# HGRN2 layer of a RetNet/S5/HGRN2 hybrid: the final output projection is woven into the last HGRN steps, and the decode heads into the second half's strips

## The reference, cut to what matters

```python
z = h @ w_in                                   # 1024 -> 4 * 1024: q, f_raw, i, g
q = silu(q)
f_gate = lower_bound + (1 - lower_bound) * sigmoid(f_raw)
log_f, k = log(f_gate), 1 - f_gate
o, s_new = hgrn2_chunkwise(q, log_f, k, i, s_hg)   # per head: s = diag(decay) s + k^T i, o = q s
o = head_rms_norm(o, norm_w) * silu(g)
x = x + o @ w_out                              # w_out1, 1024 x 1024
y = rms_norm(x, final_norm_w)
```

## Time and profile before

| | us |
|---|---|
| runs (3), median | 3449.12 |
| runs, lowest to highest | 3437.54 to 3450.01 |
| the profiled execution, its own time | 3435.53 |
| its span in the trace | 3433.7 |
| PE busy | 3118.8 (91%) |
| DVE, ACT, POOL busy | 1441.1, 1060.1, 1021.2 |

### The profile page before, as it was taken

One profiled execution on the slowest core, in us unless ns is written; L12 is line 12 of the kernel. 1 busy time (PEld: TensorE's weight loads), 2 busy tenths in 40 slices (PEclk: granted clock), 3 DMA queues, 4 the chain that ended last, 5 costly groups with the idle time before them and its releaser, 6 DMA issues. The chain is left out here.

```text
span 3433.7 us, 46623 instructions
## 1 busy us (share of the span) xinstructions
PE 3118.8 (91%) x16972; PEld 2750.7 (80%) x16972; DVE 1441.1 (42%) x2894; ACT 1060.1 (31%) x1761; POOL 1021.2 (30%) x641
## 2 busy tenths in 40 slices
PE   6999899899999688597899969999989999967799
PEld 6999899688888575497788849999978888866587
DVE  7998344214410596533300022133444444455522
ACT  4111122312211241433200020034545454588221
POOL 2232222122223472111222202344434444433021
PEclk9999999899999898799899979999989999967899
DMA  5444655455532563443422222333333333332342
GB/s 133 98 130 138 184 165 159 104 131 169 169 114 86 209 208 112 166 123 119 158 93 95 86 94 76 99 124 111 111 109 116 113 115 99 95 132 67 141 160 99
DMA packets 376296, 429.97 MB, mean 125 GB/s; under 512 B 49600, under 2 KB 318400, under 8 KB 366960
## 3 DMA queue, kind: packets, MB, share of 16 engines
q1 hardware_dynamic: 258960, 347.81, 32.4%
q10 hardware_dynamic: 117216, 80.53, 7.5%
HBM read 281.07 MB, written 151.39 MB: 126 GB/s over the span
## 5 line engine op out<-in xcount | busy, mean ns | idle before, releaser
L1114 PE MATMUL p_psum<-p_h_hi,p_w_hi 128*128 128x344 f32 (+1 forms) x1600 | 568.3, 355 | 0.0
L1114 PE MATMUL p_psum<-p_h_hi,p_w_lo 128*128 128x344 f32 (+1 forms) x1600 | 562.0, 351 | 0.0
L1114 PE MATMUL p_psum<-p_h_lo,p_w_hi 128*128 128x344 f32 (+1 forms) x1600 | 560.9, 351 | 0.0
L2328 PE MATMUL p_psum<-p_h_hi,p_w_hi 128*128 128x344 f32 (+1 forms) x1280 | 461.9, 361 | 0.0
L2328 PE MATMUL p_psum<-p_h_lo,p_w_hi 128*128 128x344 f32 (+1 forms) x1280 | 455.5, 356 | 0.0
L2328 PE MATMUL p_psum<-p_h_hi,p_w_lo 128*128 128x344 f32 (+1 forms) x1280 | 455.2, 356 | 0.0
L698 POOL CAST p_w_hi<-p_w_raw 128x1024 fp32r<-128x1024 f32 x80 | 88.9, 1112 | 821.0 <-PE p_psum L1114 685.4
L1114 PEld LDWEIGHTS p_psum<-p_h_hi,p_w_hi 128*128 128x128 f32 x1600 | 302.8, 189 | 36.7 <-issue 9.5
L1114 PEld LDWEIGHTS p_psum<-p_h_hi,p_w_lo 128*128 128x128 f32 x1600 | 302.8, 189 | 29.1
L1114 PEld LDWEIGHTS p_psum<-p_h_lo,p_w_hi 128*128 128x128 f32 x1600 | 302.8, 189 | 28.5
L2137 DVE COPY p_out<-p_psum 128x344 f32<-128x344 f32 (+1 forms) x160 | 93.4, 584 | 481.8 <-PE p_psum L2328 481.7
(11 more groups left out here) (321 smaller groups left out, 5605.7 us busy)
## 6 DMA issues: line engine op xcount, KB each, us to landing
p_w_raw<-in_w_in SPq DMA_DIRECT2D x144, 512.0 KB, 4.5
z<-p_out ACTq DMA_DIRECT2D x64, 512.0 KB, 3.5
z<-p_out SPq DMA_DIRECT2D x64, 512.0 KB, 3.2
p_raw<-z SPq DMA_DIRECT2D x32, 1024.0 KB, 5.4
rt_raw<-z SPq DMA_DIRECT2D x16, 1536.0 KB, 6.9
c_m_raw<-m SPq DMA_DIRECT2D x16, 1024.0 KB, 6.8
u_s<-p_out SPq DMA_DIRECT2D x128, 73.0 KB, 3.1
p_shared<-u_s SPq DMA_DIRECT2D x32, 292.0 KB, 5.1
```

The lines of the kernel that those rows point to most:

```text
L1114: ins = pe.matmul(bank, wv[par][:, k, :], h[:, k, c0:c0 + n], start=(k == 0 and j == 0), stop=(k == KD - 1 and j == 2))
L2328: ins = pe.matmul(bank, wv[par][:, k, :], h[:, k, c0:c0 + n], start=(k == 0 and j == 0), stop=(k == KD - 1 and j == 2))
```

## The change

The two last stages become one function; `combine` is no longer called for the second layer.

- The strips of the second half use PSUM banks 0 and 1 only, and a block waits for the eviction of the same block of the strip just before it. Banks 2 and 3 are free for the decode heads.
- The 8 decode heads move into the iterations 10 to 20, one new head in each, its parts spread over three iterations. Their states go through four buffers (the token buffers `xt` and `xn`, which the second half's prelude has left) instead of eight. DVE gets one head's work per iteration, PE its 2 transposes, 8 products into states and 8 out of them. SP loads and stores a state per iteration; before, ACT's queue stored them.
- At iteration 23 (`LAST_STRIP`) `w_out1` is loaded and split into the memory of the split tokens (`h_hi`, `h_lo`), through four row buffers: POOL makes the high parts, DVE the low parts. POOL also splits the first two input tiles.
- From iteration 25 (`OUT`) each iteration computes one tile of the output projection, `out_part(c, 0)` where strip `slot(k, 0)` was and `out_part(c, 1)` where `slot(k, 1)` was. So 9 tiles share iterations 25 to 33 with the HGRN steps and 8 follow in iterations 34 to 41. DVE's `add_out` comes after `norm_o`, ACT's `square_out` after `square_o`, DVE's `norm_out` at the end of the iteration; POOL's `split_mixed` does both parts of the input; SP loads tile c+2 and stores the result.
- `log_f` has one buffer instead of two.

```diff
+        s_state = [v[:].rearrange("p (n c) -> p n c", c=P) for v in (xt[0], xt[1], xn[0], xn[1])]
+        k_own = wrow[0:NS].rearrange("p (n c) -> p n c", c=P)
...
+        wo_hi, wo_lo = h_hi[:, :, 0:D], h_lo[:, :, 0:D]
+        wo_raw = [v[:, 0:D] for v in (out_buf[0], out_buf[1], xn[0][:], xn[1][:])]
+        m_raw, m_hi, m_lo = w_raw, w_hi, w_lo
+        xi, xo, sq = xt, xn, [o[:, 0:D] for o in out_buf]
...
+        OWN, OWN_END, OUT = 10, 20, 25
+        N_OUT = NT + 1
...
+            def load_weights(r):
+                if r >= 4:
+                    sp.wait_ge(wo_lo_done, r - 3)
+                sp.dma_start(wo_raw[r % 4], a["w_out1"][r * P:(r + 1) * P, :]).then_inc(wo_ld[r % 4], 16)
+            def load_mixed(c):
+                tile, n = out_no(c)
+                if c >= 2:
+                    sp.wait_ge(m_lo_done, c - 1)
+                if c < NT:
+                    for u in range(2):
+                        at = tile // NTH * (2 * NTH) + u * NTH + tile % NTH
+                        sp.wait_ge(mix_st[at % 2], 16 * (at // 2 + 1))
+                sp.dma_start(m_raw[c % 2][:, :, 0:n], mix["z"][tile, :, :, :] if n == P else mix["zs"])\
+                    .then_inc(m_ld[c % 2], 16)
+                if c >= 2:
+                    sp.wait_ge(sum_done, c - 1)
+                sp.dma_start(xi[c % 2][0:n, :], x_in["x"][tile, :, :] if n == P else x_in["s"]).then_inc(xi_ld[c % 2], 16)
+            def store_out(c):
+                tile, n = out_no(c)
+                sp.wait_ge(y_done, c + 1)
+                sp.dma_start(x_out["x"][tile, :, :] if n == P else x_out["s"], xo[c % 2][0:n, :]).then_inc(y_st[c % 2], 16)
...
+                    if k == LAST_STRIP and e == 0:
+                        sp.wait_ge(blk_done, blocks_to(N_STRIPS))
+                        for e4 in range(4):
+                            sp.wait_ge(s_st[e4], 32)
                         for par in range(2):
                             sp.wait_ge(stored[par], store_count(N_STRIPS + par))
-                        for h in range(HH):
...
+                        sp.wait_ge(w_lo_done, N_STRIPS)
+                        for r in range(4):
+                            load_weights(r)
+                        for c in range(2):
+                            load_mixed(c)
+                        for r in range(4, KD):
+                            load_weights(r)
+                    if e == 1 and out_tile(k) is not None and out_tile(k) + 2 < N_OUT:
+                        if out_tile(k) + 2 == NT:
+                            sp.wait_ge(d_stored, 16)
+                        load_mixed(out_tile(k) + 2)
+                    if e == 0 and out_tile(k - 1) is not None:
+                        store_out(out_tile(k - 1))
...
+                if k == LAST_STRIP:
+                    pool.wait_ge(blk_done, blocks_to(N_STRIPS))
+                    for r in range(KD):
+                        pool.wait_ge(wo_ld[r % 4], 16 * (r // 4 + 1))
+                        pool.tensor_copy(wo_hi[:, r, :], wo_raw[r % 4]).then_inc(wo_hi_done, 1)
+                        if r < 2:
+                            split_mixed(r)
+                elif out_tile(k) is not None and out_tile(k) + 2 < N_OUT:
+                    split_mixed(out_tile(k) + 2)
...
+            def square_out(c):
+                par, n = c % 2, out_no(c)[1]
+                act.wait_ge(sum_done, c + 1)
+                if c == 0:
+                    act.wait_ge(wo_lo_done, KD)
+                act.activation(sq[par][0:n, :], xo[par][0:n, :], ACT.Square, scale=D ** -0.5,
+                               accum_out=stat[par][0:n, 0:1]).then_inc(ysq_done, 1)
+                act.wait_ge(ysq_done, c + 1)
+                act.activation(stat[par][0:n, 1:2], stat[par][0:n, 0:1], ACT.Sqrt, bias=eps[0:n, :]).then_inc(yrms_done, 1)
...
+            for k in range(OUT + N_OUT + 1):
                 if k == BEFORE_B:
                     prelude(1)
                 if 0 <= k - 1 < N_HG:
                     values(k - 1)
-                if k >= 2:
...
+                if 0 <= k - 2 < N_HG:
                     square_o(k - 2)
+                if out_tile(k - 1) is not None:
+                    square_out(k - 1 - OUT)
                 if k < N_HG:
                     exps(k)
                 if 0 <= k - 1 < N_HG:
                     turned_keys(k - 1)
                 if k + 1 < N_HG:
-                    log_gates(k + 1)
...
+                    log_gates(k + 1, k == OWN - 2)
...
-                    dve.tensor_copy(out_buf[par][:, c0:c0 + n], ps[:, b if hf == 0 else 2 * par + b, 0:n])\
+                    dve.tensor_copy(out_buf[par][:, c0:c0 + n], ps[:, b, 0:n])\
...
+            def own_keys(h):
+                dve.wait_ge(own_mm, h + 1)
+                if h:
+                    dve.wait_ge(kv_mm, 2 * h)
+                dve.tensor_copy(i_own[:], ps_own[0:NS, 0, :])
+                dve.tensor_tensor(k_own, bcast(ps_own[0:NS, 1, :], 1, NS), bcast(ident[0:NS, 0:NS], 2, P), ALU.mult)\
+                    .then_inc(own_done, 1)
+                s = s_state[h % 4]
+                dve.wait_ge(s_ld[h % 4], 16 * (h // 4 + 1))
+                dve.tensor_tensor(s, s, bcast(own_f[:, h // H4, h % H4, :], 2, P), ALU.mult).then_inc(dec_done, 1)
+            def add_own(h, c):
+                s = s_state[h % 4][:, 4 * c:4 * c + 4, :]
+                dve.wait_ge(dec_done, h + 1)
+                dve.wait_ge(kv_mm, 2 * h + c + 1)
+                dve.tensor_tensor(s, s, ps_kv, ALU.add).then_inc(kv_done, 1)
...
+            for k in range(OUT + N_OUT + 1):
                 if k == BEFORE_B:
                     prelude(1)
-                if k >= 2:
+                if 0 <= k - 2 < N_HG:
                     take_state(k - 2)
                 if k < N_HG:
                     relative(k)
-                if k >= 2:
+                if 0 <= k - 2 < N_HG:
                     norm_o(k - 2)
+                if own_head(k - 1) is not None:
+                    add_own(k - 1 - OWN, 0)
...
+                if out_tile(k - 1) is not None:
+                    add_out(k - 1 - OUT)
                 evict(slot(k, 0), (0, 1, 2))
                 if 0 <= k - 1 < N_HG:
                     mask_scores(k - 1)
-                if k >= 2:
+                if 0 <= k - 2 < N_HG:
                     mix_o(k - 2)
                 if k < N_HG:
                     queries(k)
...
+                if own_head(k - 1) is not None:
+                    add_own(k - 1 - OWN, 1)
+                if own_head(k) is not None:
+                    own_keys(k - OWN)
...
                 evict(slot(k, 1), (0, 1))
                 if k + 1 < N_HG:
                     sum_logs(k + 1)
                 evict(slot(k, 1), (2,))
-
...
+                if k == LAST_STRIP:
+                    for r in range(KD):
+                        dve.wait_ge(wo_hi_done, r + 1)
+                        dve.tensor_tensor(wo_lo[:, r, :], wo_raw[r % 4], wo_hi[:, r, :].bitcast(F32), ALU.subtract)\
+                            .then_inc(wo_lo_done, 1)
+                if out_tile(k - 1) is not None:
+                    norm_out(k - 1 - OUT)
...
-                    if hf == 0:
-                        before = blocks_to(g - 1) + b + 1 if g else 0
-                    else:
-                        before = blocks_to(g - 2) + b + 1 if s >= 2 else blocks_to(N_P1)
+                    before = blocks_to(g - 1) + b + 1 if g else 0
                     if before:
                         pe.wait_ge(ev_done, before)
-                    bank = ps[:, b if hf == 0 else 2 * par + b, 0:n]
+                    bank = ps[:, b, 0:n]
...
+            def out_part(c, half):
+                par, n = c % 2, out_no(c)[1]
+                if half == 0:
+                    pe.wait_ge(wo_lo_done, KD)
+                    pe.wait_ge(m_lo_done, c + 1)
+                    if c == 0:
+                        pe.wait_ge(ev_done, blocks_to(N_STRIPS))
+                    if c == 1:
+                        pe.wait_ge(dmix_done, 1)
+                    if c >= 2:
+                        pe.wait_ge(sum_done, c - 1)
+                for k in range(KD):
+                    for j, (m, w) in enumerate(((m_hi, wo_hi), (m_hi, wo_lo), (m_lo, wo_hi))):
+                        ins = pe.matmul(ps[0:n, 2 * par + half, :], m[par][:, k, 0:n],
+                                        w[:, k, half * BLK:(half + 1) * BLK],
+                                        start=(k == 0 and j == 0), stop=(k == KD - 1 and j == 2))
+                if half:
+                    ins.then_inc(mm_done, 1)
...
+            for k in range(OUT + N_OUT):
                 if k == BEFORE_B:
                     prelude(1)
                 strip(slot(k, 0))
+                if out_tile(k) is not None:
+                    out_part(k - OUT, 0)
                 if 0 <= k - 1 < N_HG:
                     turn_k(k - 1)
                     scores(k - 1)
-                if k >= 2:
+                if 0 <= k - 2 < N_HG:
```

(13 more changed lines are left out.)

349 lines of the change are left out of this document (195 added, 154 removed).

## The result

The kernel after takes **3384.17 us** (median of 4 runs, 3382.68 to 3388.75). The kernel before, timed beside it on the same chip, takes 3443.33 (3437.01 to 3450.01). The ratio is 0.983 (95% interval 0.9803 to 0.9857). The forecast was 3384, in 3354 to 3418. The profiled executions tell less of a gain than the medians: their spans are 3386.9 and 3433.7 us, 46.8 apart against 59 between the medians. The executions of the kernel before come near 3434 or near 3447 us (10 and 14 of the 24 that were timed beside the first experiments), the profiled one is of the first kind, and the traces put the difference into one stretch, the decode heads' products behind the last step.

A forecast was written before the change was run, and what follows sets the result against it. PE was taken to bound iterations with strips, ACT those without, and PE the last stage. Saving 99.7 less 34 for heads gave about 65: 3370.5 us profiled, plus 13.6 to the median, 3384; range 3354 to 3418.

The forecast's parts named there:

- From iteration 23 to the end: Weights, iterations with tiles, remaining tiles and tail: 325 us where the kernel before takes 424.7, saving 99.7.
- The sum of the loop: Iterations 27 to 30: DVE to ACT and back, 9.0 + 1.5 + 12.25 = 22.75 us, with PE's 18.8 inside.
- friction: Iterations 27 to 30: 0.75 us added to the loop's 22.75, giving 23.5 each.
- The last low part: Sign: DVE's last low part of the output weights ends near 3043 + 34 = 3077 us.
- The rule: DVE instructions with two SBUF inputs and GpSimd instructions reading SBUF exclude each other; up to 2.3 us per tile iteration.
- The heads: Iterations before 23: each of 8 heads costs PE 4.1 us under strips, plus 1 for final transposes: +34 us.
- the 13.6 us: Added to the forecast profiled execution, 3370.5 us, because the median of the runs is that much higher: 3384.
- Late input: Rival: in five tile iterations the step's input lands late behind the residual's load, 5 us more each: 3409; chance 0.15.
- DVE against POOL: Rival: DVE and POOL exclude each other in the tile iterations' chain, 12 us in five: 3396; chance 0.12.
- PE as all there is: Rival: tile iterations take only PE's 18.8 us and the weights hide: 3354; chance 0.10.
- The heads' waits: Rival: heads under strips keep the decode stage's PE waits, 59 us instead of 34: 3409; chance 0.04.
- The banks: Rival: 64 second-half blocks wait 0.8 us each for evictions, 51 us: 3435, no change; chance 0.04, half-way 0.02.

The follow-up runs named there:

- spread weights: Kernel after with the output weights' rows 0 to 3 split in iteration 23, rows 4 to 7 and the input splits in 24: 3385.25 us, ratio 0.9839.
- late splits: Kernel after with POOL's two input splits behind its eight casts of weights in iteration 23 instead of between them: 3380.31 us, ratio 0.9836.
- The late heads: Kernel after with the second half of a head's state products and the next head's transposes behind the second strip: 3362.72 us, ratio 0.976.
- the squaring is late: Kernel after with SP's order changed, ACT's squaring of a tile one iteration later and DVE's `norm_out` behind the queries: 3370.44 us, ratio 0.9803.
- The paddings: Eight needless transposes per iteration: kernel before, ahead of `turn_o` 0.9966, ahead of `turn_i` 0.9971; kernel after, ahead of `turn_i` 0.9849.

## Why the prediction came out right, step by step

**From iteration 23 to the end: right.** The forecast was 325 us, counted from PE's last transposes of iteration 22; the same stretch is 3057.0 (PE's L2546 above, with its 0.60) to 3386.9, 329.9 us, against 424.7 before. To the first tile 52.2 us (50 forecast), from there to the last add 270.2 (268), the tail 7.5 (7). The pieces inside:

- Iterations 27 to 30 take 22.35 us each (marks from 3161.07 to 3250.45, four of them), not 23.5. The sum of the loop, 22.75, was nearer than the sum with its friction of 0.75; `norm_out` took 1.28 us and not 1.56. No two instructions held each other up in this chain; POOL's subtraction fell beside DVE work that reads PSUM (3179.85 above).
- Iterations 25 and 26 take 24.0 and 22.3, not 20 and 19: 7.3 us more, where the former point gained 4.6. Iteration 25 runs at a clock of 0.93 and the closed loop holds from 26 on.
- The last low part was to come near 3077 and came at 3094. Of the 17 us, 14 are the heads, which moved everything by 48 instead of 34; the other 3 are covered by the scan, which took 6.80 us beside POOL's splits instead of 1.37; some of that the forecast had in its slower last low parts. The rule that the prediction quoted from the Trainium skill, page SBUF — State Buffer, section "Who interferes with whom", agrees with the trace at a place for which the prediction hadn't used it; in the iterations with tiles, for which it had been kept as a rival, it cost nothing. The runs with spread weights and late splits show both sides of it.

**The heads: the mechanism right, the size off.** The term "8 x 4.1 = 33, and 1 for the final transposes: +34" measured 52.2 us between the marks of iterations 7 and 23 (48.0 from the start of the span). A head takes 4.5 us at 2.4 GHz, some 36 in all. What was missing is the clock, and the sentence that failed is "I take 34, since the strips beside the heads run at 2.4 GHz". The iterations with a head run at 0.91, and one with a spell of 6.8 us pays 37.4 - 34.3 = 3.1 us for it. The kernel before already paid 185.4 / 6 - 29.8 = 1.1 an iteration for its own spells; the iteration of 29.8 us at a clock of 1.00, from which the forecast took its clock, was one of those without. Counted between the marks of iterations 7 and 23, the kernel after has eight spells of 6.8 us and five of 3.4, the kernel before one and nine (the low clock at the very end of iteration 22 left out); at 3.2 and 1.6 us each that is 33.6 against 17.6. So of the 52.2 us some 36 are the heads' work, 2 more than forecast, and 16 are the clock, which the forecast put at nothing. The late heads, at 34.3 us and a clock of 1.00, show that this is what the clock took.

**Why 3384 was met all the same.** The forecast of the saving, 65 us against the profiled execution, was 18 too high (46.8 by the spans). But the forecast of the median added the 13.6 us by which the profiled execution of before lay under its median, as if the kernel after kept that distance. It doesn't: the distance is about what the decode heads' stretch takes more at the lower clock (48.4 us against 34.7), and the change removes that stretch. After's profiled execution (1.8 us over its span, 3388.7) lies 4.5 above its own median. The two errors, 18 and 18, cancel, and that is luck; with one of them alone the forecast would have been 18 us off, still with the time inside a range of this width.

**The rivals.** Late input: refuted by the run with SP's order changed and by ACT, which waits only for the add. DVE against POOL: real, but at the weights. PE as all there is: false in the kernel after, true once the squaring is late (18.7 us, with a spell 20.2). The heads' waits: PE never idles there; what comes on top of the 36 us of work is the clock, 16 us, of the 25 that this rival would have added. The banks: 1.0002.

**What stays open.** Why the chip lowers the clock in one iteration and not in another of the same work. The paddings speak for the moment at which the short stretch comes; the late heads changed moment and stretch at once and don't tell the two apart. Open too is why the decode heads' stretch of the kernel before runs at 0.89 in one execution and 0.62 in another, and whether an edit far ahead of it, such as a padding, shifts how often either comes.

## What to carry to other kernels

Work laid under a PE-bound stretch costs its PE time plus what it does to TensorE's clock; look at the granted clock of the iteration before and after, and try the new short products at another place of the iteration: here moving half of them was worth 0.7%. A profiled execution that lies off the median of its kernel has a reason in some stretch; before that distance is carried over to a changed kernel, look whether the change keeps the stretch. Where an engine's queue holds work of two chains (steps and tiles), put the piece that closes a loop between two engines one iteration later than seems natural: 22.35 became 18.7 us, or 19.6 on average with PE's spells. And where GpSimd's subtraction of two SBUF operands lay beside VectorE's scan, low parts or `relative`, these took two to five times as long; moving it moved most of the loss and gained nothing that the timing shows.

## What the runs showed of the hardware that was not expected

- Eight iterations with 0.9 us of needless transposes in each took 245.7 us in all, 4 us less than without (249.8), since those of 30.7 us kept a granted clock of 1.00 where five of the eight without fell to 1.2 GHz for 3.4 us and one for 6.8. With the transposes at another place six of the eight kept it, and the sum was 250.4. The Trainium skill, page TensorE: Matmul & The Clock Gate, part "The HAM clock gate", says that the monitor behind the clock runs free and isn't aligned with the program; that in one kernel iterations of the same work have a spell or none agrees with it.
- In the iterations with strips the spells came in two lengths, 3.4 and 6.8 us, priced 1.6 and 3.2 us, while PE was busy all the time.
- The same 256 matmuls of the decode heads took 34.7 us at a granted clock of 0.89 and 48.4 at 0.62, in executions of kernels that differ only in their strips' PSUM banks.
- A DVE scan of four 128 x 128 operands took 1.37 us alone, 2.45 beside POOL's casts and 6.80 beside its casts and subtractions. Two low parts took 2.33 us and 5.26 beside the splits.
